# The projection's epilogue: head scales in the rotary tables, squares and normalising straight from PSUM

## The chip, the cores and the metric

The kernel runs on one core of a Trainium2 chip, in float32 throughout. The metric is the device time of one execution in microseconds (us). TensorE is called PE here, its weight loads PEld, VectorE DVE, ScalarE ACT, GpSimd POOL, and SyncE, which only issues DMAs, SP.

## The reference

One layer of an encoder over 1024 tokens and 16 learned meta tokens (1040 rows of 1024 features). What matters here is its first part:

```python
u = _rmsnorm(h, g_attn[l])
proj = u @ w_in[l]                      # 1024 x 2304
qa, ka, va, qd, kd, vd = [proj[..., offs[i]:offs[i + 1]] for i in range(6)]
qa = _rope(_rmsnorm(qa.reshape(B, L, SWA_HQ, SWA_DH), g_q_swa[l]), pos)
ka = _rope(_rmsnorm(ka.reshape(B, L, SWA_HKV, SWA_DH), g_k_swa[l]), pos)
# the same for the 16 q heads and 16 k heads of width 32 of the differential attention
def _rmsnorm(x, g): return x * rsqrt(mean(x * x, -1) + eps) * g       # per head
def _rope(x, pos):  return concat([x1 * cos - x2 * sin, x2 * cos + x1 * sin])   # x1, x2: halves of a head
```

After it come windowed attention, differential attention, the output projection, a router and 32 experts of which each token takes 4. None of that is touched.

## The kernel before, in words

`project` is the first of six stages; a barrier of all engines ends it. Its columns are taken in five groups: 0 is V of the differential attention (512 columns), 1 its Q (512), 2 its K (512), 3 the window attention's Q (512), 4 its K and V (256). An item is one group of columns of one tile of 128 rows; there are 43, numbered 0 to 42 in order: group 0 items 0 to 8, group 1 items 9 to 16, group 2 items 17 to 25, group 3 items 26 to 33, group 4 items 34 to 42. The ninth tile holds the 16 meta rows, and groups 1 and 3 leave it out.

Every product is made of three in single-pass float32: hi x hi, hi x lo, lo x hi (L474 to L476), eight k-tiles, so 24 matmuls an item into one of four PSUM banks `pp`. ACT casts weights to `w_in_hi` (L249) and DVE subtracts to get `w_in_lo` (L327), from four staging buffers that SP fills. The split weights lie in a ring of RING = 14 slots; two groups need 16, so the last LATE = 2 k-tiles of a group can be split only once the group before has used its first ones. `late(i)` says which k-tiles are split beside item i: the first five or six items of a group take one k-tile of the next group each, and a group's first item takes its own late ones too.

An item of groups 1 to 4 then goes through the epilogue, in iterations m of a loop that each engine runs in the same order:

- m = i + 1: ACT copies PSUM to `pr` (L268); POOL squares it into `sq` (L422); DVE sums the squares by head (L343); ACT takes the root (L273); DVE takes the reciprocal (L349) and multiplies `pr` by it into `qn` (L352).
- then POOL multiplies `qn` by the head gains (L430) and, in two halves, by the sine into `t2` (L437). One iteration later on DVE, `rotate` multiplies it in two halves by the cosine into `t1` (L364) and subtracts and adds the halves into `ro` (L370, L371).
- m = i + 3: PE transposes `ro` into `ptq` (L463), up to four blocks, after the products of item m.
- m = i + 4: ACT casts it to `qk_hi` (L282), DVE subtracts to get `qk_lo` (L379), SP stores both (L197).

Each engine works its list in order. DVE's order within an iteration is `qk_lo`, weight tiles, sums, reciprocal, `qn`, `rotate` of the item before. PE waits for `proj_out` before it writes a bank again, four items later.

Of the kernel before, what the change touches and what calls it, by code (L numbers as in the profile page):

```python
# [26 lines left out]
P = 128  # L27
# [48 lines left out]
def project(nc, a, v_all, qk_dram):  # L76

    with ExitStack() as ctx:  # L80
        sb = lambda n, s, d=F32: ctx.enter_context(nc.sbuf_tensor(n, s, d))
        used = []

        def sem(n):
            used.append(nc.alloc_semaphore(n + "_in"))
            return used[-1]

        T = NT + 1
        RAW, RING, GW = 4, 14, 512
        LATE = 2 * KC - RING  # L90
# [22 lines left out]
        ident = sb("ident1", [P, P])  # L113
        pr = sb("pr", [P, 2, GW])
        sq = sb("sq", [P, GW])
# [22 lines left out]
        sq_done, hs_done, hstd_done = sem("head_squares"), sem("head_sums"), sem("head_std")  # L138
        qn_done, gain_done, t1_done, t2_done, ro_done = (sem("qn_done"), sem("gain_done"), sem("t1_done"),
                                                        sem("t2_done"), sem("rotated"))  # L140
        qk_ps, hi_done, lo_done = sem("qk_transposed"), sem("hi_done"), sem("lo_done")
        qk_stored = [sem(f"qk_stored{i}") for i in range(2)]
        dve_chain = sem("dve_chain1")

        def heads(i):

            g, t = items[i]
            c0, c1, at, d, gain = groups[g]
            w = 2 * DH if c0 == KA else c1 - c0
            return rows[t], w, d, gain, (0 if d == DH else 2 * 32)  # L150

        def split_heads(ap, d):
# [21 lines left out]
        def _(sp):  # L174
# [27 lines left out]
            for p in range(RAW):  # L202
                load_w(p)
            load_x(1)
            sp.dma_start(rope[:, 0:NT, :], a["rope"][0:SEQ, :].rearrange("(t p) n -> p t n", p=P)
                         ).then_inc(const_landed, 16)
            sp.dma_start(rope[0:N_META, NT, :], a["rope"][SEQ:KEYS, :]).then_inc(const_landed, 16)
            for i, n in enumerate(("g_q_swa", "g_k_swa")):
# [6 lines left out]
            for p in range(KC, KC + RAW):  # L215
                load_w(p)
            for m in range(NI + 5):
                if m + 3 < T:
                    load_x(m + 3)
                for p in late(m) if m < NI else ():  # L220
                    if p + RAW < NP:
                        load_w(p + RAW)
                if FH <= m - 4 < NI:
                    store(m - 4)
            for i in range(2):
# [3 lines left out]
        def _(act):  # L229
# [27 lines left out]
            def evict(i):  # L257
                g, t = items[i]
                r, w = rows[t], groups[g][1] - groups[g][0]
                act.wait_ge(proj_ps, i + 1)  # L260
                if g == 0:
                    act.copy(v_all[0:r, t, 128:640], pp[0:r, i % 4, 0:512]).then_inc(proj_out, 1)
                else:
                    h = i - FH
                    if h >= 2:
                        act.wait_ge(qn_done, h - 1)
                        act.wait_ge(sq_done, h - 1)
                    act.copy(pr[0:r, h % 2, 0:w], pp[0:r, i % 4, 0:w]).then_inc(proj_out, 1)  # L268

# [21 lines left out]
            norm(1)  # L291
            for m in range(NI + 5):
                if 1 <= m <= NI:
                    evict(m - 1)
                if FH <= m - 4 < NI:
                    high_qk(m - 4)
                if m < NI:
                    g, t = items[m]
                    for p in late(m):
                        high_w(p)  # L300
                    if g == 0:
                        if t + 1 < T:
                            high_u(t + 1)
                        if t + 2 < T:
                            norm(t + 2)
                if FH <= m - 1 < NI:
                    head_std(m - 1)

        @block.vector
        def _(dve):  # L310
            step = chained(dve, dve_chain)
            dve.memset(eps[:, :], EPS).then_inc(consts_set, 1)

# [31 lines left out]
            def normalise(i):  # L345
                r, w, d = heads(i)[0:3]
                h, nh = i - FH, w // d
                dve.wait_ge(hstd_done, h + 1)
                step(dve.reciprocal(hr[0:r, 0:nh], hr[0:r, 0:nh]))  # L349
                if h >= 2:  # L350
                    dve.wait_ge(t2_done, 2 * (h - 1))
                dve.tensor_tensor(split_heads(qn[0:r, h % 2, 0:w], d), split_heads(pr[0:r, h % 2, 0:w], d),  # L352
                                  hr[0:r, 0:nh].unsqueeze(2).broadcast_to((r, nh, d)), ALU.mult).then_inc(qn_done, 1)

            def rotate(i):
                r, w, d, _, c = heads(i)
                h, nh, t = i - FH, w // d, items[i][1]
                dve.wait_ge(gain_done, h + 1)
                if h >= 1:
                    dve.wait_ge(ro_done, 2 * h)  # L360
                q, x, y, o = (split_halves(b, d) for b in (qn[0:r, h % 2, 0:w], t1[0:r, 0:w], t2[0:r, 0:w], ro[0:r, h % 2, 0:w]))
                cos = rope[0:r, t, c:c + d // 2].unsqueeze(1).broadcast_to((r, nh, d // 2))
                for s in range(2):
                    ins = dve.tensor_tensor(x[:, :, s, :], q[:, :, s, :], cos, ALU.mult)  # L364
                ins.then_inc(t1_done, 1)
                dve.wait_ge(t1_done, h + 1)
                dve.wait_ge(t2_done, 2 * (h + 1))
                if h >= 2:
                    dve.wait_ge(qk_ps, h - 1)
                dve.tensor_tensor(o[:, :, 0, :], x[:, :, 0, :], y[:, :, 0, :], ALU.subtract).then_inc(ro_done, 1)  # L370
                dve.tensor_tensor(o[:, :, 1, :], x[:, :, 1, :], y[:, :, 1, :], ALU.add).then_inc(ro_done, 1)  # L371

# [17 lines left out]
            dve.tensor_scalar(gaind[:, 0, :], gaind[:, 0, :], DQ ** -0.5, None, ALU.mult).then_inc(consts_set, 1)  # L390
            for m in range(NI + 5):
                if FH <= m - 4 < NI:
                    low_qk(m - 4)
                if m < NI:
# [8 lines left out]
                if FH <= m - 1 < NI:  # L403
                    head_sums(m - 1)
                    normalise(m - 1)
                if FH <= m - 2 < NI:
                    rotate(m - 2)

        @block.gpsimd
        def _(pool):  # L410
            pool.wait_ge(consts_set, 2)
            pool.wait_ge(const_landed, 16 * 8)

            def squares(i):
                r, w = heads(i)[0:2]
                h = i - FH
                pool.wait_ge(proj_out, i + 1)
                if h >= 1:
                    pool.wait_ge(hs_done, h)
                if items[i][0] == NG - 1:  # L420
                    pool.tensor_copy(v_all[0:r, items[i][1], 0:128], pr[0:r, h % 2, 128:256])
                pool.tensor_tensor(sq[0:r, 0:w], pr[0:r, h % 2, 0:w], pr[0:r, h % 2, 0:w], ALU.mult).then_inc(sq_done, 1)  # L422

            def gain_and_sine(i):
                r, w, d, gain, c = heads(i)
                h, nh, t = i - FH, w // d, items[i][1]
                pool.wait_ge(qn_done, h + 1)
                v = split_heads(qn[0:r, h % 2, 0:w], d)
                table = gains if d == DH else gaind
                pool.tensor_tensor(v, v, table[0:r, gain, :].unsqueeze(1).broadcast_to((r, nh, d)), ALU.mult).then_inc(gain_done, 1)  # L430
                pool.wait_ge(gain_done, h + 1)
                if h >= 1:
                    pool.wait_ge(ro_done, 2 * h)
                q, y = split_halves(qn[0:r, h % 2, 0:w], d), split_halves(t2[0:r, 0:w], d)
                sin = rope[0:r, t, c + d // 2:c + d].unsqueeze(1).broadcast_to((r, nh, d // 2))
                for s in range(2):
                    pool.tensor_tensor(y[:, :, s, :], q[:, :, 1 - s, :], sin, ALU.mult).then_inc(t2_done, 1)  # L437

            for m in range(FH + 1, NI + 5):
                if FH <= m - 1 < NI:  # L440
                    squares(m - 1)
                if FH <= m - 2 < NI:
                    gain_and_sine(m - 2)

        @block.tensor
        def _(pe):
# [36 lines left out]
            transpose_u(0)  # L483
            for m in range(NI + 3):
                if m < NI:
# [3 lines left out]
                    if m >= 4:  # L489
                        pe.wait_ge(proj_out, m - 3)  # L490
                    products(m, 0, KC // 2)
                    if g == 0 and t + 1 < T:
                        transpose_u(t + 1)
                    products(m, KC // 2, KC)
                if FH <= m - 3 < NI:
                    transpose_qk(m - 3)

# [1655 lines left out]
```

## Time and profile before

| | |
|---|---|
| time, median of 3 runs | 2607.39 us (2606.91 to 2609.02) |
| time of the profiled execution | 2607.83 us |
| its span | 2606.2 us |
| PE, DVE, ACT, POOL busy in it | 2335.1, 1924.8, 1451.3, 477.3 us |
| mean granted clock of TensorE | 0.945 of full |
| first 282 us (the projection): PE, DVE, ACT, POOL busy | 246.79, 203.44, 88.12, 126.74 us |

Matmuls overlap in the pipeline, so that PE's busy time doesn't say how near it is to its own rate; the start-to-start time of items in the timeline does. A wait is put down to the instruction that released it last. Instructions of one engine overlap a little, so the time that one takes from its engine is read from start to start.

### The profile page before, as it was taken

How to read it: one execution, taken by the hardware profiler on the slowest of the kernel's cores; microseconds unless marked ns; L12 is line 12 of the kernel's file. 1: busy time of each engine (PE TensorE's matmuls, PEld its weight loads, DVE VectorE, ACT ScalarE, POOL GpSimd, SP SyncE). 2: the span in 40 equal slices, each digit the busy share in tenths (PEclk: the TensorE clock that was granted, in tenths of full speed). 3: DMA queues.
4: the chain of work that ended last, by engine and by line, in shares of the span. 5: the costliest groups of instructions: out<-in, count | busy, mean ns of one | idle time of the engine just before them, and what ended most of it. 6: DMA issues, size and time to landing. Idle time of an engine off the chain costs nothing. (4 is left out here: it accounts for less than half of the span.)

```text
span 2606.2 us, 35142 instructions
## 1 busy us (share of the span) xinstructions
PE 2335.1 (90%) x10673; PEld 1742.3 (67%) x10674; DVE 1924.8 (74%) x2425; ACT 1451.3 (56%) x1694; POOL 477.3 (18%) x546
## 2 busy tenths in 40 slices
PE   6999698999979579999899889999999999988964
PEld 5767565555558457777778677777777777777741
DVE  4699456999956368787775687777777777788767
ACT  4222355888832166676654475656565567667540
POOL 0466100111102311221110011212121111122120
PEclk9999798999989789999999899999999999999985
DMA  4233712332016398797976688877887679799868
GB/s 155 59 108 94 161 40 80 66 66 50 17 45 114 93 337 324 282 348 271 360 254 223 236 318 294 305 256 267 287 311 261 240 277 356 260 353 360 293 242 361
DMA packets 259924, 574.86 MB, mean 221 GB/s; under 512 B 29201, under 2 KB 61329, under 8 KB 254721
## 3 DMA queue, kind: packets, MB, share of 16 engines
q1 hardware_dynamic: 237296, 534.92, 60.3%
q0 software_dynamic: 21056, 34.49, 3.7%
q10 hardware_dynamic: 1488, 4.39, 0.4%
q8 instruction: 46, 0.75, 0.1%
q14 instruction: 38, 0.30, 0.0%
HBM read 548.17 MB, written 60.15 MB: 233 GB/s over the span
## 5 line engine op out<-in xcount | busy, mean ns | idle before, releaser
L1732 DVE TENSOR_TENSOR wlo<-raw,whi 128x2048 fp32r<-128x2048 f32 x387 | 880.6, 2287 | 293.2 <-ACT whi L1628 285.9
L1628 ACT CAST whi<-raw 128x2048 fp32r<-128x2048 f32 x387 | 730.9, 1909 | 227.1 <-PE gl_ps L1900 138.5
L1902 PE MATMUL gl_ps<-whi,xt_hi 128*128 128x512 f32 x1056 | 420.9, 399 | 41.6 <-PEq L1946 24.6
L1904 PE MATMUL gl_ps<-whi,xt_lo 128*128 128x512 f32 x1056 | 414.3, 392 | 0.0
L1903 PE MATMUL gl_ps<-wlo,xt_hi 128*128 128x512 f32 x1056 | 414.1, 392 | 0.0
L1902 PEld LDWEIGHTS gl_ps<-whi,xt_hi 128*128 128x128 f32 x1056 | 199.9, 189 | 93.6 <-issue 25.5
L1904 PEld LDWEIGHTS gl_ps<-whi,xt_lo 128*128 128x128 f32 x1056 | 200.1, 190 | 43.3
L1903 PEld LDWEIGHTS gl_ps<-wlo,xt_hi 128*128 128x128 f32 x1056 | 200.4, 190 | 40.1
L1902 PE MATMUL y_ps<-whi,ht_hi 128*128 128x512 f32 x512 | 215.2, 420 | 0.0
L1903 PE MATMUL y_ps<-wlo,ht_hi 128*128 128x512 f32 x512 | 208.7, 408 | 0.0
L1904 PE MATMUL y_ps<-whi,ht_lo 128*128 128x512 f32 x512 | 208.3, 407 | 0.0
L1562 POOL DMA_INDIRECT xg<-v_dram,idn x67 | 113.6, 1695 | 483.4 <-PE t_ps L1872 403.6
L704 DVE CUSTOM_DVE_ANT_0 e<-s_ps,zero,meta_nm 128x1024 f32<-128x1024 f32 x128 | 163.4, 1277 | 11.8 <-DVE dsb L719 9.9
L1900 PE MATMUL gl_ps<-wlo,xt_hi 128*64 128x512 f32 x416 | 164.7, 396 | 0.0
L1899 PE MATMUL gl_ps<-whi,xt_hi 128*128 128x512 f32 x416 | 162.5, 391 | 0.1
L1602 POOL DMA_INDIRECT y_dram<-ys,idc x64 | 64.0, 1000 | 528.4 <-ACT ys L1672 380.4
L632 ACT ACTIVATE e<-e,nm 128x1040 f32<-128x1040 f32 x128 | 149.1, 1165 | 8.8 <-DVE nm L704 7.9
L474 PE MATMUL pp<-w_in_hi,ut_hi 128*128 128x512 f32 (+3 forms) x344 | 134.6, 391 | 11.2 <-DVE w_in_lo L327 8.8
L817 PE MATMUL o_ps<-pt,v_all 128*64 128x512 f32 (+1 forms) x288 | 139.3, 607 | 0.0
L475 PE MATMUL pp<-w_in_lo,ut_hi 128*128 128x512 f32 (+3 forms) x344 | 130.7, 380 | 0.0
L476 PE MATMUL pp<-w_in_hi,ut_lo 128*128 128x512 f32 (+3 forms) x344 | 129.6, 377 | 0.0
L1649 ACT CAST ht_hi<-t_ps 128x512 fp32r<-128x512 f32 x92 | 45.7, 529 | 128.8 <-PE t_ps L1892 128.4
(262 smaller groups left out, 3954.3 us busy)
## 6 DMA issues: line engine op xcount, KB each, us to landing
raw<-in_w_mlp SPq DMA_DIRECT2D x390, 1024.0 KB, 6.1
b<-in_b_mlp SPq DMA_DIRECT2D x33, 1024.0 KB, 7.7
yk<-y_dram SPq DMA_DIRECT2D x7, 2048.0 KB, 24.7
k_st<-qk_dram SPq DMA_DIRECT2D x32, 260.0 KB, 7.5
xs<-in_x SPq DMA_DIRECT2D x16, 512.0 KB, 4.6
w_in_raw<-in_w_in SPq DMA_DIRECT2D x32, 256.0 KB, 2.9
q_st<-qk_dram SPq DMA_DIRECT2D x32, 256.0 KB, 6.7
qk_dram<-qk_hi SPq DMA_DIRECT2D x24, 256.0 KB, 2.6
```

Of the source, the lines that this page charges most:

```text
L474: pe.matmul(out, ut_hi[:, k, cols(i)], whi[:, s, 0:w], start=(k == 0), stop=False)
L475: pe.matmul(out, ut_hi[:, k, cols(i)], wlo[:, s, 0:w], start=False, stop=False)
L632: act.activation(e[:, n % 2, i, :], e[:, n % 2, i, :], ACT.Exp, bias=nm[:, k:k + 1], scale=-1.0, accum_out=total[:, n % 16, i:i + 1]).then ...
L704: dve.tensor_tensor_reduce(e[:, n % 2, i, 0:SEQ], S(i), zero[:, :], -1.0, meta_nm[:, (n // NT) % 2, at:at + 1], ALU.add, ALU.min, nm[:, k: ...
L817: ins = pe.matmul(o_ps[DV:P, :], vt, pt[0:r, g % 2, c, :], start=(c == 0), stop=(c == 8), skip_group_check=True)
L1628: act.copy(whi[:, k % SPL, :], raw[:, k % RAW, :]).then_inc(hi_done, 1)
L1732: dve.tensor_tensor(wlo[:, k % SPL, :], raw[:, k % RAW, :], whi[:, k % SPL, :].bitcast(F32), ALU.subtract).then_inc(lo_done, 1)
L1899: ins = pe.matmul(bank, xh[:, 1, kc, :], hi, start=start, stop=stop, skip_group_check=True)
L1900: ins = pe.matmul(bank[0:FEW], xh[:, 1, kc, 0:FEW], lo, start=False, stop=stop, skip_group_check=True)
L1902: pe.matmul(bank, xh[:, half, kc, :], hi, start=start, stop=False, skip_group_check=True)
L1903: pe.matmul(bank, xh[:, half, kc, :], lo, start=False, stop=False, skip_group_check=True)
L1904: return pe.matmul(bank, xl[:, half, kc, :], hi, start=False, stop=stop, skip_group_check=True)
```

## The change

The copy to `pr` and the gain product are gone. ACT squares the PSUM bank itself into `sq`, and copies V of the last group from PSUM. DVE multiplies the bank by the reciprocals. POOL builds, once for a group, tables over all nine tiles: cosine times gain and sine times gain, for each head position (four products a table; those of groups 1 and 2 ahead of the loop, those of 3 and 4 behind the sine product of the first item of group 2 and 3). A cosine and a sine product then are one instruction each over all 512 columns, and the subtraction and addition pick the halves. `rotate` moves to the start of DVE's iteration; transposes, casts and stores come one iteration earlier. PE takes `qn` of item m - 4 as the sign that a bank is free. The tables take 9216 bytes a partition, `pr` gave back 4096, and RING goes from 14 to 13, with which LATE becomes 3. DVE sets the 16-row tile of the cosines to zero first, and SP's load into it waits for that.

```diff
...
-RAW, RING, GW = 4, 14, 512
+RAW, RING, GW = 4, 13, 512
...
-pr = sb("pr", [P, 2, GW])
+table = sb("rope_gain", [P, 2, 2, T * DH])
...
-qn_done, gain_done, t1_done, t2_done, ro_done = (sem("qn_done"), sem("gain_done"), sem("t1_done"),
-                                                sem("t2_done"), sem("rotated"))
+qn_done, table_done, t1_done, t2_done, ro_done = (sem("qn_done"), sem("table_done"), sem("t1_done"),
+                                                 sem("t2_done"), sem("rotated"))
...
+rope_set = sem("rope_set")
...
+def rope_gain(i, part):
...
+    r, w, d = heads(i)[0:3]
+    g, t = items[i]
+    return table[0:r, g % 2, part, t * d:(t + 1) * d].unsqueeze(1).broadcast_to((r, w // d, d))
...
+    sp.wait_ge(rope_set, 1)
...
-    for m in range(NI + 5):
+    for m in range(NI + 4):
...
-        if FH <= m - 4 < NI:
-            store(m - 4)
+        if FH <= m - 3 < NI:
+            store(m - 3)
...
-            h = i - FH
-            if h >= 2:
-                act.wait_ge(qn_done, h - 1)
-                act.wait_ge(sq_done, h - 1)
-            act.copy(pr[0:r, h % 2, 0:w], pp[0:r, i % 4, 0:w]).then_inc(proj_out, 1)
+            h, w = i - FH, heads(i)[1]
+            if h >= 1:
+                act.wait_ge(hs_done, h)
+            act.activation(sq[0:r, 0:w], pp[0:r, i % 4, 0:w], ACT.Square).then_inc(sq_done, 1)
+            if g == NG - 1:
+                act.copy(v_all[0:r, t, 0:128], pp[0:r, i % 4, 128:256]).then_inc(proj_out, 1)
...
-    for m in range(NI + 5):
+    for m in range(NI + 4):
...
-        if FH <= m - 4 < NI:
-            high_qk(m - 4)
+        if FH <= m - 3 < NI:
+            high_qk(m - 3)
...
 def _(dve):
...
+    dve.memset(rope[:, NT, :], 0.0).then_inc(rope_set, 1)
...
-            dve.wait_ge(t2_done, 2 * (h - 1))
-        dve.tensor_tensor(split_heads(qn[0:r, h % 2, 0:w], d), split_heads(pr[0:r, h % 2, 0:w], d),
+            dve.wait_ge(t2_done, h - 1)
+            dve.wait_ge(t1_done, h - 1)
+        dve.tensor_tensor(split_heads(qn[0:r, h % 2, 0:w], d), split_heads(pp[0:r, i % 4, 0:w], d),
...
     def rotate(i):
-        r, w, d, _, c = heads(i)
-        h, nh, t = i - FH, w // d, items[i][1]
-        dve.wait_ge(gain_done, h + 1)
+        r, w, d = heads(i)[0:3]
+        h = i - FH
+        dve.wait_ge(qn_done, h + 1)
+        dve.wait_ge(table_done, 4 * items[i][0])
...
-        q, x, y, o = (split_halves(b, d) for b in (qn[0:r, h % 2, 0:w], t1[0:r, 0:w], t2[0:r, 0:w], ro[0:r, h % 2, 0:w]))
-        cos = rope[0:r, t, c:c + d // 2].unsqueeze(1).broadcast_to((r, nh, d // 2))
-        for s in range(2):
-            ins = dve.tensor_tensor(x[:, :, s, :], q[:, :, s, :], cos, ALU.mult)
-        ins.then_inc(t1_done, 1)
+        dve.tensor_tensor(split_heads(t1[0:r, 0:w], d), split_heads(qn[0:r, h % 2, 0:w], d), rope_gain(i, 0), ALU.mult
+                          ).then_inc(t1_done, 1)
+        x, y, o = (split_halves(b, d) for b in (t1[0:r, 0:w], t2[0:r, 0:w], ro[0:r, h % 2, 0:w]))
...
-        dve.wait_ge(t2_done, 2 * (h + 1))
+        dve.wait_ge(t2_done, h + 1)
...
-        dve.tensor_tensor(o[:, :, 0, :], x[:, :, 0, :], y[:, :, 0, :], ALU.subtract).then_inc(ro_done, 1)
-        dve.tensor_tensor(o[:, :, 1, :], x[:, :, 1, :], y[:, :, 1, :], ALU.add).then_inc(ro_done, 1)
+        dve.tensor_tensor(o[:, :, 0, :], x[:, :, 0, :], y[:, :, 1, :], ALU.subtract).then_inc(ro_done, 1)
+        dve.tensor_tensor(o[:, :, 1, :], x[:, :, 1, :], y[:, :, 0, :], ALU.add).then_inc(ro_done, 1)
...
-    for m in range(NI + 5):
-        if FH <= m - 4 < NI:
-            low_qk(m - 4)
+    for m in range(NI + 4):
+        if FH <= m - 2 < NI:
+            rotate(m - 2)
+        if FH <= m - 3 < NI:
+            low_qk(m - 3)
...
-        if FH <= m - 2 < NI:
-            rotate(m - 2)
...
 def _(pool):
...
-    def squares(i):
-        r, w = heads(i)[0:2]
-        h = i - FH
-        pool.wait_ge(proj_out, i + 1)
-        if h >= 1:
-            pool.wait_ge(hs_done, h)
-        if items[i][0] == NG - 1:
-            pool.tensor_copy(v_all[0:r, items[i][1], 0:128], pr[0:r, h % 2, 128:256])
-        pool.tensor_tensor(sq[0:r, 0:w], pr[0:r, h % 2, 0:w], pr[0:r, h % 2, 0:w], ALU.mult).then_inc(sq_done, 1)
...
-    def gain_and_sine(i):
-        r, w, d, gain, c = heads(i)
-        h, nh, t = i - FH, w // d, items[i][1]
+    pool.wait_ge(rope_set, 1)
...
+    def make_table(g):
...
+        d, gain = groups[g][3:5]
+        c, n = (0 if d == DH else 2 * 32), d // 2
+        gains_of = (gains if d == DH else gaind)[:, gain, :]
+        for part in range(2):
+            out = table[:, g % 2, part, 0:T * d].rearrange("p (t s n) -> p t s n", t=T, s=2)
+            for s in range(2):
+                half = gains_of[:, s * n:(s + 1) * n].unsqueeze(1).broadcast_to((P, T, n))
+                pool.tensor_tensor(out[:, :, s, :], rope[:, :, c + part * n:c + (part + 1) * n], half, ALU.mult
+                                   ).then_inc(table_done, 1)
...
+    def sine(i):
+        r, w, d = heads(i)[0:3]
+        h, g = i - FH, items[i][0]
...
-        v = split_heads(qn[0:r, h % 2, 0:w], d)
-        table = gains if d == DH else gaind
-        pool.tensor_tensor(v, v, table[0:r, gain, :].unsqueeze(1).broadcast_to((r, nh, d)), ALU.mult).then_inc(gain_done, 1)
-        pool.wait_ge(gain_done, h + 1)
+        pool.wait_ge(table_done, 4 * g)
...
-        q, y = split_halves(qn[0:r, h % 2, 0:w], d), split_halves(t2[0:r, 0:w], d)
-        sin = rope[0:r, t, c + d // 2:c + d].unsqueeze(1).broadcast_to((r, nh, d // 2))
-        for s in range(2):
-            pool.tensor_tensor(y[:, :, s, :], q[:, :, 1 - s, :], sin, ALU.mult).then_inc(t2_done, 1)
...
-    for m in range(FH + 1, NI + 5):
-        if FH <= m - 1 < NI:
-            squares(m - 1)
-        if FH <= m - 2 < NI:
-            gain_and_sine(m - 2)
+        pool.tensor_tensor(split_heads(t2[0:r, 0:w], d), split_heads(qn[0:r, h % 2, 0:w], d), rope_gain(i, 1), ALU.mult
+                           ).then_inc(t2_done, 1)
+        if i == first_of[g] and 2 <= g < NG - 1:
+            make_table(g + 1)
...
+    make_table(1)
+    make_table(2)
+    for i in range(FH, NI):
+        sine(i)
...
-    for m in range(NI + 3):
+    for m in range(NI + 2):
...
-                pe.wait_ge(proj_out, m - 3)
+                h = m - 4 - FH
+                if h < 0:
+                    pe.wait_ge(proj_out, m - 3)
+                else:
+                    pe.wait_ge(qn_done, h + 1)
+                    if items[m - 4][0] == NG - 1:
+                        pe.wait_ge(proj_out, FH + m - 3 - first_of[NG - 1])
...
-        if FH <= m - 3 < NI:
-            transpose_qk(m - 3)
+        if FH <= m - 2 < NI:
+            transpose_qk(m - 2)
```

## Rows read from the trace of the kernel before

**Rows 1.** The page, parts 1 and 2: busy time, and the clock in 40 slices.

```profile
PE 2335.1 (90%) x10673; PEld 1742.3 (67%) x10674; DVE 1924.8 (74%) x2425; ACT 1451.3 (56%) x1694; POOL 477.3 (18%) x546
...
PEclk9999798999989789999999899999999999999985
```

**Rows 2.** Stretches: length, busy time of PE, PEld, DVE, ACT, POOL, clock, DMA share, GB/s.

```profile
120.00:140.00 20.00, 18.05 (x78) 14.05 (x77) 18.67 (x28) 5.74 (x13) 12.59 (x12) 0.93 0.37 106
...
240.00:260.00 20.00, 15.88 (x110) 15.30 (x109) 18.27 (x37) 5.64 (x14) 13.18 (x21) 0.83 0.36 104
```

**Rows 3.** Waits of PE, 82.9 to 282 us: total us, times, longest.

```profile
PE pp L474 <- DVE w_in_lo L327: 8.8, 5, 4.1
PE ptq L463 <- DVE ro L371: 4.7, 5, 2.6
```

**Rows 4.** Timeline of PE: start us, length us, instruction, idle before it.

```profile
82.91 0.40 PE L474 MATMUL pp<-w_in_hi,ut_hi 128*128 128x512 f32 x1
88.47 0.40 PE L474 MATMUL pp<-w_in_hi,ut_hi 128*128 128x512 f32 x1
...
135.77 0.51 PE L474 MATMUL pp<-w_in_hi,ut_hi 128*128 128x512 f32 x1 [1.79 <-DVE w_in_lo L327]
...
157.66 0.49 PE L474 MATMUL pp<-w_in_hi,ut_hi 128*128 128x512 f32 x1
...
163.67 0.48 PE L474 MATMUL pp<-w_in_hi,ut_hi 128*128 128x512 f32 x1
...
247.63 0.58 PE L474 MATMUL pp<-w_in_hi,ut_hi 128*128 128x256 f32 x1 [4.12 <-DVE w_in_lo L327]
...
254.70 0.36 PE L474 MATMUL pp<-w_in_hi,ut_hi 128*128 128x256 f32 x1
...
257.99 0.36 PE L474 MATMUL pp<-w_in_hi,ut_hi 128*128 128x256 f32 x1
...
260.94 0.37 PE L474 MATMUL pp<-w_in_hi,ut_hi 128*128 128x256 f32 x1
...
275.54 0.74 PE L463 MATMUL ptq<-ident,ro 128*128 128x128 f32 x2
```

**Rows 5.** Timeline of DVE over one period, from reduce to reduce.

```profile
157.65 0.67 DVE L343 TENSOR_REDUCE hs<-sq 128x16 f32<-128x512 f32 x1
...
158.98 0.69 DVE L352 TENSOR_TENSOR qn<-pr,hr 128x512 f32<-128x512 f32 x1
159.59 2.70 DVE L364 TENSOR_TENSOR t<-qn,rope_sb 128x256 f32<-128x256 f32 x2
162.33 0.42 DVE L370 TENSOR_TENSOR ro<-t 128x256 f32<-128x256 f32 x1
...
163.01 0.68 DVE L379 TENSOR_TENSOR qk_lo<-ptq,qk_hi 128x512 fp32r<-128x512 f32 x1
163.61 0.90 DVE L327 TENSOR_TENSOR w_in_lo<-w_in_raw,w_in_hi 128x512 fp32r<-128x512 f32 x1
164.44 0.67 DVE L343 TENSOR_REDUCE hs<-sq 128x16 f32<-128x512 f32 x1
```

**Rows 6.** Timelines: POOL in that period, and DVE's weight tile while POOL idles.

```profile
159.22 1.36 POOL L422 TENSOR_TENSOR sq<-pr 128x512 f32<-128x512 f32 x1 [0.89 <-ACT pr L268]
160.54 1.48 POOL L430 TENSOR_TENSOR qn<-qn,gaind_sb 128x512 f32<-128x512 f32 x1
...
33.69 0.69 DVE L327 TENSOR_TENSOR w_in_lo<-w_in_raw,w_in_hi 128x512 fp32r<-128x512 f32 x1 [1.50 <-ACT w_in_hi L249]
```

**Rows 7.** Groups of ACT by form, 0 to 300 us: busy us, mean ns.

```profile
L268 ACT COPY pr<-pp 128x512 f32<-128x512 f32 x24 | 13.7, 573 | 9.4 <-PE pp L476 9.4
L235 ACT ACTIVATE us<-xs 128x1024 f32<-128x1024 f32 x8 | 8.5, 1059 | 2.1 <-DMA xs<-in_x 2.1
```

**Rows 8.** A group of POOL by form, and the timeline of the last `qk_lo`.

```profile
L430 POOL TENSOR_TENSOR qn<-qn,gains_sb 128x128 f32<-128x128 f32 x8 | 3.9, 483 | 0.0
...
281.42 0.17 DVE L379 TENSOR_TENSOR qk_lo<-ptq,qk_hi 128x16 fp32r<-128x16 f32 x1 [1.16 <-ACT qk_hi L282]
```

## The prediction

> **What bounds the kernel now.** I read the engines' shares first: PE 90%, DVE 74% of the whole span [rows 1]. Those are averages over stages, and the change touches only the first one, the projection, so the next view is the busy time in stretches. In 120 to 140 us DVE is busy 18.67 of 20.00 us, ACT only 5.74, and PE loses 2 us; in 240 to 260 us DVE has 18.27 and PE 15.88, with the clock down to 0.93 and 0.83 of full [rows 2]. So DVE is full and PE has holes. The waits of PE between 82.9 and 282 us say which holes: 8.8 us in 5 waits for `w_in_lo` of DVE L327 and 4.7 us in 5 for `ro` of DVE L371 [rows 3]. Both releasers are DVE instructions: the stage is bound by DVE in its epilogue, and PE pays at the group boundaries, where fresh weights have to be split behind it.
>
> PE's own pace comes from the timeline. An item without head transposes takes 88.47 - 82.91 = 5.56 us, one with four transposes 163.67 - 157.66 = 6.01, a 256-column item 257.99 - 254.70 = 3.29 with four transposes and 260.94 - 257.99 = 2.95 with one [rows 4]. DVE's period comes from two successive reduces: 164.44 - 157.65 = 6.79 us [rows 5]. 6.79 against 6.01 is why DVE lags. PE has four PSUM banks of slack and so feels it only where it catches up: the waits of 1.79 and 4.12 us at 135.77 and 247.63, for instance [rows 4].
>
> **What PE could gain.** Items 9 to 42 and their stalls take 275.54 - 82.91 = 192.63 us [rows 4]. The same PE work in the new order (transposes one item earlier, so from item 11 on) at PE's pace: 2 x 5.56 + 23 x 6.01 + 2 x 3.29 + 7 x 2.95 = 11.12 + 138.23 + 6.58 + 20.65 = 176.58. All that DVE costs PE is 16.05 us. That is more than the 13.5 us of named waits [rows 3], since the granted clock also falls in the two stretches that hold the waits ending at 135.77 and 247.63 [rows 2, 4].
>
> **The change part by part.** DVE's period now, start to start [rows 5]: reduce to `qn` 158.98 - 157.65 = 1.33 (with the square root on ACT in it), `qn` 0.61, the two cosine products 162.33 - 159.59 = 2.74, the two `ro` 163.01 - 162.33 = 0.68, `qk_lo` 0.60, `w_in_lo` 164.44 - 163.61 = 0.83; sum 6.79.
> - *Normalising straight from PSUM.* The row for a 512-column DVE read of PSUM, `qk_lo`, occupies 0.68, and `qn` from SBUF 0.69 [rows 5]: no difference, 0.61 stays. The Trainium skill, "VectorE: DVE Perf Modes", Rules for kernel authors, speaks against this edit: copy PSUM to SBUF first if many operations follow. Here each bank gets two reads by DVE/ACT, and the two rows just named are equal, so that rule would add nothing measurable at this type.
> - *Squares from POOL to ACT, the copy `pr` removed.* On ACT one 512-column pass replaces another. Bounds: 573 ns, the copy from PSUM, and 1059 ns, a Square of 1024 columns [rows 7]; I take 600. ACT is under 30% busy [rows 2], and the square is ready sooner than by copy plus POOL's 1.36 [rows 6]. In the last group a 128-column copy of V is added behind it, under the 0.57 of the wide copy; ACT's idle hides both. Without that cover the square would cost 0.03 us more an item than the copy, and the V copy at most 9 x 0.57 = 5 us.
> - *Cosine product.* Two 256-column products become one of 512. Alone such a product costs 0.61 (as `qn`), the pair of halves 0.68 (as the two `ro`); the present pair takes 2.74 because POOL is active beside it: POOL runs 159.22 to 162.02 [rows 6], and the 0.31 us left after that is nearly half of 0.68. So in 2.43 us beside POOL DVE did about 0.37 us of work, a rate of 0.15. POOL now has one sine product, of the form of its present gain product, 1.48 us [rows 6], and both start at the same `qn`. Estimate: 1.48 us at that rate gives 0.22, the other 0.39 follow: 1.87, say 1.9. Lower end 0.61, upper 2.74; nearer the middle since POOL's 2.8 us of work beside it shrink to about 1.5. The following `ro` wait for POOL's product, which is done by then.
> - *Low weights.* The L327 in rows 5 takes 0.90 beside POOL's sine products of the item before, alone 0.69 [rows 6]; POOL is now idle at that time, so the slot shrinks from 0.83 to 0.62.
> - New period: 1.33 + 0.61 + 1.9 + 0.68 + 0.60 + 0.62 = 5.74 us, 5.12 without a weight tile. Both are under 6.01: **PE becomes the bound**. The removed gain product (POOL 1.48) and one sine product are on no path of the middle.
>
> The Trainium skill, "GPSIMD Engine Reference", Key points, says the SBUF interfaces are shared with VectorE, with contention when a VectorE instruction has two SBUF inputs. By that rule, the trace agrees in the 2.74 us pair; `qk_lo` and the new `qn`, with one input in PSUM, would be spared, which changes no term of the sum.
>
> **What is late next.** With T the end of an item's products, DVE starts `qk_lo` at about T + 1.35 (transposes 0.45, ACT square and hi cast 0.6 each less overlap), and `ro` is complete at T + 1.35 + 5.74 = T + 7.1. PE asks for it after two more items, at T + 12.0: 4.9 us of room. Against it: a group's first item now has four weight tiles (LATE 3, was 2), 3 x 0.62 = 1.9 us; and in groups 2 and 3 POOL builds the next table, four products of 288 columns, by 1.48/512 a column 0.83 us each, 3.3 us together, in which DVE's two-input instructions crawl: 1 to 2.5 us. Sum at most 4.4: inside the room, thinly; if it isn't, each excess shows as a wait of PE for `ro`. The late tiles: PE needs the first of three at T + 0.45 + 15 x 0.23 = T + 3.9, DVE has it at T + 2.6. In the last group (products half as long) it is needed at T + 2.2 and the third at T + 2.9, and they come at T + 2.4 and T + 3.3: 0.5 us, and `ro` of the item before about 0.4 late. I charge 0.9 for this and 1.1 for leftover lag: 16.05 - 2.0 = **14 us** from the loop. The tables of groups 1 and 2 are built near 30 us, long before their use at 95 us; the memset, the wait for it on SP (ahead of it in time by 4 us) and the stores behind it cost nothing. SP's queue sees the same DMAs in the same order, stores one iteration earlier.
>
> **The tail** from the last product to the last `qk_lo` is 281.42 + 0.17 - 275.54 = 6.05 us [rows 4, 8]. Out of it go POOL's gain product (483 ns [rows 8]), one of two sine products, and the copy-then-square pair becomes one pass. That is 0.5, some 0.3 (a quarter of the work of the 483 ns one in two halves, with its fixed part) and up to 0.7; I take 1.5 (bounds 0 and 2.5, as the last hi cast may wait for its buffer's store instead).
>
> Sum: 14 + 1.5 = 15.5 us. The profiled execution took 2607.83 (span 2606.2 and 1.6 around it), the median is 0.44 lower: 2607.4 - 15.5 = **2591.9 us**. Later stages start earlier and are otherwise the same.
>
> **Rivals.**
> 1. *DVE still sets the pace.* If the cosine product beside POOL stays at 2.74, the period is 6.58. For: the only such row. Against: POOL's work beside it halves. DVE then lags 0.6 per weighted item plus 1.9 at boundaries and up to 2.5 for a table, past the room of 4.9 by 2 to 3 us in three groups: gain 15.5 - 8 = 7.5, time 2600.
> 2. *The clock spells stay.* The two dips amount to (1 - 0.93) x 20 and (1 - 0.83) x 20 us of lost clock [rows 2], 1.4 + 3.4 = 4.8. If they come whether PE waits or not, the gain is 10.7: 2596.7. For: the page shows the clock at nine tenths in slices all over the run, busy ones too [rows 1]. Against: here both dips share their stretch with a wait, and nothing in the change adds a pause of PE.
> 3. *Given back later*: the shift of 15 us changes where later dips fall or a DMA bounds the next stage's start. Time within 0.2%, 2603 to 2612.
> 4. *Slower.* DVE, in order, now waits for POOL's sine product of the same item before `ro`, with `qk_lo` and weights queued behind; PE waits for those. It decides from the point where product plus wait exceeds 2.74 + 0.2 = 2.94 (period back at 6.79, with one more late tile), and it costs over 5 us net only from about 3.2 on for all 25 wide items: 25 x 0.26 = 6.5, time 2614. POOL would need twice its 1.48 row for it.
>
> **How the numbers follow.** Forecast 0.57 (own range 2588 to 2595), a yet larger gain 0.04, rival 1 0.16, rival 2 0.13, rival 3 0.06, rival 4 0.04. Range 2587 to 2601. A change under 0.2% (5.2 us) can't be told from none: faster 0.90, same 0.06, slower 0.04.
>
> **What would show it.** Right: item pace of 6.01 from item 11 to 33, no wait of PE for L327 in groups 2 and 3, ACT Square near 0.6, the 512-column cosine product between 1.6 and 2.1, POOL's sine product near 1.5, the stage's last `qk_lo` near 266. Wrong: PE waits for `ro` in each group, a cosine product of 2.7, or a stage end 15 us earlier with the total unmoved.

## The result and the profile after

The changed kernel takes 2591.18 us (median of 4 runs, 2587.86 to 2591.83), the kernel before beside it 2608.2 (2606.91 to 2609.14): ratio 0.9933, 95% interval 0.9915 to 0.995. The forecast was 2591.9 with a range of 2587 to 2601. The median fell by 17.0 us; the profiled spans are 2606.2 and 2589.4 us, 16.8 us apart.

The stretches that held PE's holes [rows 2], in the kernel after: PE is busy throughout, DVE two thirds, and the clock stays at full.

```profile
120.00:140.00 20.00, 20.00 (x94) 16.33 (x93) 13.65 (x26) 6.75 (x14) 5.39 (x3) 1.00 0.46 131
240.00:260.00 20.00, 20.00 (x172) 19.65 (x173) 12.20 (x53) 6.68 (x29) 3.96 (x7) 1.00 0.30 87
```

All waits of PE from 82.9 to 265 us, where there were 8.8 us on weights and 4.7 on `ro` [rows 3]. Of these 3.3 us, 2.6 lie behind the last product (0.21 and 2.41, at 261.27 and 264.01 us). Of the 4.7 before, 3.5 did (2.62 and 0.89, at 278.89 and 280.11 us), so that inside the items the waits fell from 10.0 to 0.7 us:

```profile
PE ptq L473 <- DVE ro L382: 3.3, 3, 2.4
```

PE's timeline, at the places that answer to [rows 4]: the first products of items 9 and 10, of items 22 and 23, of 34, 35 and 36, and the first transposes behind the last product.

```profile
83.22 0.40 PE L484 MATMUL pp<-w_in_hi,ut_hi 128*128 128x512 f32 x1
88.78 0.40 PE L484 MATMUL pp<-w_in_hi,ut_hi 128*128 128x512 f32 x1
...
160.38 0.49 PE L484 MATMUL pp<-w_in_hi,ut_hi 128*128 128x512 f32 x1
...
166.39 0.49 PE L484 MATMUL pp<-w_in_hi,ut_hi 128*128 128x512 f32 x1
...
232.59 0.37 PE L484 MATMUL pp<-w_in_hi,ut_hi 128*128 128x256 f32 x1
...
236.14 0.36 PE L484 MATMUL pp<-w_in_hi,ut_hi 128*128 128x256 f32 x1
...
240.31 0.36 PE L484 MATMUL pp<-w_in_hi,ut_hi 128*128 128x256 f32 x1
...
260.79 0.27 PE L473 MATMUL ptq<-ident,ro 128*128 128x128 f32 x1
```

Items 11 to 33 pass at 6.01 us, PE's own pace. Only the entry of the last group is slower: 3.55 and 4.17 us for items 34 and 35, where 3.29 is the pace. The 0.7 us of waiting that is left inside the items is there, for `ro` at 239.90 us.

DVE's period in the kernel after, and POOL beside it (answers to [rows 5, 6]): the bracket is the idle time before an instruction.

```profile
158.97 0.68 DVE L354 TENSOR_REDUCE hs<-sq 128x16 f32<-128x512 f32 x1
...
160.31 0.69 DVE L364 TENSOR_TENSOR qn<-pp,hr 128x512 f32<-128x512 f32 x1
161.03 0.69 DVE L374 TENSOR_TENSOR t<-qn,rope_gain 128x512 f32<-128x512 f32 x1
162.97 0.43 DVE L381 TENSOR_TENSOR ro<-t 128x256 f32<-128x256 f32 x1 [1.25 <-POOL t L445]
```

```profile
161.08 1.80 POOL L445 TENSOR_TENSOR t<-qn,rope_gain 128x512 f32<-128x512 f32 x1 [4.08 <-DVE qn L364]
```

From `qn` to the next with a weight tile between them it is 160.31 - 154.43 = 5.88 us, without one 5.28. Squares on ACT from PSUM take 0.60:

```profile
L276 ACT ACTIVATE sq<-pp 128x512 f32<-128x512 f32 x24 | 14.4, 599 | 47.4 <-PE pp L486 47.3
```

Where the 16.8 us come from, by the two timelines:

| stretch | before, us | after, us | less |
|---|---|---|---|
| start to item 9 | 82.91 | 83.22 | -0.31 |
| item 9 to the end of the products | 192.63 | 177.57 | 15.06 |
| tail, to the end of the last `qk_lo` | 6.05 | 3.88 | 2.17 |
| to the first matmul of the window attention | 16.41 | 17.21 | -0.80 |
| the rest | 2308.2 | 2307.5 | 0.7 |

Next to nothing was given back. The two small losses lie within what single profiles differ by: in those below item 9 begins anywhere from 81.1 to 84.6 us, and the stretch from the last `qk_lo` to the first matmul of the window attention takes 16.4 to 17.8 us.

### The profile page after: what moved, and what is told of

It is laid out like the page before. It is cut to its first block and busy times, and to the rows that moved or that the text cites. A ratio compares the mean times of both kernels' runs of the same rounds, so it can differ in the third digit from the quotient of the medians.

```text
span 2589.4 us, 34999 instructions
## 1 busy us (share of the span) xinstructions
PE 2328.6 (90%) x10673; PEld 1739.0 (67%) x10674; DVE 1874.4 (72%) x2392; ACT 1452.9 (56%) x1703; POOL 408.1 (16%) x451
```

## The experiments

The later stages, whose code is the same in all of these, differ by up to 6 us between profiles (2305.3 us from the first matmul of the window attention to the end in tables_only, 2311.2 in sine_twice), so the measure is the stage alone, from the first product of item 9 to the end of the last `qk_lo`, each from its one profiled execution. The ratio is to the kernel before as it ran beside each. Its median was 2605.12 us beside psum_only, tables_only, old_order and ring14, 2606.41 beside the next four and 2607.82 beside own_first and after_again, so medians of different groups can't be compared to the microsecond:

| kernel | stage, us | median, us | ratio to before, 95% interval |
|---|---|---|---|
| before | 198.68 | 2608.20 | |
| changed | 181.45 | 2591.18 | 0.9915 to 0.995 |
| psum_only | 182.85 | 2592.99 | 0.9939 to 0.9968 |
| tables_only | 183.43 | 2590.24 | 0.9928 to 0.9956 |
| old_order | 182.04 | 2590.29 | 0.993 to 0.9959 |
| ring14 | 181.17 | 2593.51 | 0.9941 to 0.9969 |
| reduce_once_more | 191.27 | 2600.53 | 0.9969 to 0.9988 |
| sine_twice | 208.62 | 2615.65 | 1.0023 to 1.0048 |
| pe_pause | 194.64 | 2603.57 | 0.9984 to 1.0003 |
| lo_first14 | 183.25 | 2593.93 | 0.994 to 0.9974 |
| own_first | 180.50 | 2589.90 | 0.9916 to 0.9941 |
| after_again | 181.60 | 2591.29 | 0.9924 to 0.9949 |

**psum_only**, one half of the change on the kernel before (the edit shortened; RING stays 14):

```diff
-act.copy(pr[0:r, h % 2, 0:w], pp[0:r, i % 4, 0:w])
+act.activation(sq[0:r, 0:w], pp[0:r, i % 4, 0:w], ACT.Square)
-dve.tensor_tensor(qn, pr, reciprocals)     # POOL's squares go too
+dve.tensor_tensor(qn, pp, reciprocals)
```

> The kernel before with one half of the change: ACT squares the PSUM bank, DVE normalises from it, POOL loses the squares; gain product, sine and cosine halves, RING 14 and the order of the iterations stay as before. Theory (PE is the bound once DVE's period is under 6.01 us): the cosine pair shares the ports with one POOL product instead of two, so DVE's period falls from 6.79 to 1.33 + 0.61 + about 1.95 + 0.68 + 0.60 + 0.83 = 6.0 us and most of the 16 us goes: 2593 to 2597. Rival (the gain is the sum of the two halves, each in proportion to the DVE or POOL work it removes): about half, 2599 to 2601. The first theory also says that the two halves alone add up to clearly more than the 16.8 us of both together.

The median lies at the lower end of the range expected. 15.8 of the 17.2 us of the stage are gone, with the gain product and the halves still there. The cosine pair takes 1.84 us instead of 2.70 [rows 5], beside one POOL product (160.46 to 161.85 us), and ends 0.28 us after it:

```profile
160.29 1.84 DVE L364 TENSOR_TENSOR t<-qn,rope_sb 128x256 f32<-128x256 f32 x2
```

**tables_only**, the other half (tables, whole products; `pr`, POOL's squares and the old order stay; RING 13):

> The kernel before with the other half: gain folded into tables, cosine and sine as one product each (RING 13, LATE 3), but copy to pr, squares on POOL and the old order of the iterations. Theory: the cosine product waits for POOL's square (about 1.0 us) and the weight tile for part of the sine product; period 1.33 + 0.61 + 1.6 + 0.68 + 0.60 + up to 1.1 = 5.9 us, again just under PE's 6.01: 2593 to 2598. Rival (in proportion): 2599 to 2601. If this half did nothing, 2608.

15.3 us are gone. The median, 2590.24, lies 2.8 us under the range expected, which was counted from a kernel before of 2607; beside this run it took 2605.12, 14.9 us more than this kernel. The halves alone give 31.1 us, together 17.2: each brings DVE to about PE's pace, and below that nothing more is to be had. The "in proportion" rival fell in both. DVE and then POOL in this kernel:

```profile
157.56 1.53 DVE L372 TENSOR_TENSOR t<-qn,rope_gain 128x512 f32<-128x512 f32 x1
...
160.41 1.48 DVE L336 TENSOR_TENSOR w_in_lo<-w_in_raw,w_in_hi 128x512 fp32r<-128x512 f32 x1
```

```profile
157.19 1.36 POOL L432 TENSOR_TENSOR sq<-pr 128x512 f32<-128x512 f32 x1 [2.04 <-ACT pr L276]
160.06 1.28 POOL L453 TENSOR_TENSOR t<-qn,rope_gain 128x512 f32<-128x512 f32 x1 [1.51 <-DVE ro L380]
```

The cosine product starts 0.37 us into POOL's square and ends 0.54 after it; the weight tile starts 0.35 into the sine product and ends 0.55 after it. So a DVE instruction with two SBUF inputs that meets a running POOL product does nearly all its work after that one ends. Its period with a weight tile is 6.20 us here, over PE's 6.01, but 4.79 without one, and PE waits only 1.1 us for weights: the room of the pipeline absorbs it.

**old_order**, the changed kernel with `rotate` back at the end of the iteration and transposes one later:

> The changed kernel with the old order: rotate at the end of DVE's iteration, transposes, casts and stores one iteration later. DVE doesn't wait for POOL's sine product then. Theory (PE is the bound, DVE's wait of 1.24 us an item lies inside its slack): loop unchanged at about 177.5 us, tail longer by up to 1.5 us, 2591 to 2593.5. Rival (the reorder was what gained): 2597 or more. Rival (DVE's waits cost something): under 2589.

The stage is 0.6 us longer, but the loop didn't stay as expected. The reorder did two things that nearly cancel. From the last product to the last `qk_lo` this kernel takes 5.46 us where the changed one takes 3.88, so the reorder saved 1.58 us in the tail. From item 9 to the end of the products it takes 176.58 us where the changed one takes 177.57: item 35 passes at 3.28 us instead of 4.17, and PE has no wait inside the items. Here DVE doesn't wait for POOL ahead of `ro`, so the rival that its waits cost something was right by that 0.9 us of item 35. The median lies 0.7 us under the range expected, beside a kernel before that was also faster. POOL's sine product, which now starts when DVE stands idle (it waits for ACT's cast until 160.51 us), takes 1.28 us instead of 1.80:

```profile
159.29 1.28 POOL L445 TENSOR_TENSOR t<-qn,rope_gain 128x512 f32<-128x512 f32 x1 [4.21 <-DVE ro L382]
```

**ring14**, RING 14 and LATE 2:

> The changed kernel with RING 14, LATE 2, as the kernel before had it. Theory: the late tile costs only in the last group, where DVE lags by one tile of 0.4 us: 0.3 to 0.8 us less than the change, 2590 to 2591.5. Rival (late tiles are a cost at every boundary): 2 us less or more, 2589 and below.

The stage is 0.28 us shorter, all of it in item 34 (3.27 us instead of 3.55), just under the 0.3 to 0.8 expected. The median, 2593.51, is above the range expected: in its profile the later stages took 2310.1 us with the same code, 2307.5 in the changed kernel. This is why the stage is the measure.

**reduce_once_more**, to find how much room DVE has:

```diff
+dve.tensor_reduce(spare[0:r, 0, 0:w // d], split_heads(sq[0:r, 0:w], d), AX.X, ALU.add)
 dve.tensor_reduce(hs[0:r, 0:w // d], split_heads(sq[0:r, 0:w], d), AX.X, ALU.add).then_inc(hs_done, 1)
```

> The changed kernel with one spare reduce of 0.61 us an item on DVE. In the changed kernel DVE's period is 5.88 us with a weight tile and 5.28 without (its trace), so over the 25 wide items it needs 25 x 5.28 + 19 tiles x 0.61 + 5 x 0.4 + 2.4 for the tables = 148 us, and PE 150. Theory (PE is the bound by a slack of only some 2 us, and PE has about 5 us of room once): 15.2 us more on DVE cost 15.2 - 2 - 5 = 8 us, up to 12 with the clock: 2598 to 2604, with PE waits for w_in_lo and ro back at the group boundaries. Rival (PE bound with ample slack): under 2593.

9.8 us more in the stage for about 15 us of work on the wide items, and PE's waits inside the items are back:

```profile
PE pp L486 <- DVE w_in_lo L339: 5.2, 2, 2.6
PE ptq L475 <- DVE ro L384: 1.2, 4, 0.4
```

These are 6.4 of the 9.8 us; the rest is about what two stretches of 3.4 us at half the clock cost, 1.7 each (see pe_pause). So the changed kernel lies close to the edge. About 5 of the 15 us cost nothing; how much could be added before the first microsecond is lost, no run shows.

**sine_twice**, POOL's product made twice, the first into a spare tile:

> The changed kernel with POOL's sine product made twice (the first into a spare tile), so that DVE waits for POOL longer. Theory (DVE's and POOL's products exclude each other and DVE stands in the wait with everything behind it): the time from qn to ro grows by 1.2 to 1.3 us, DVE's period to 7.1 with a weight tile, 32 us more over 25 wide items less 7 of slack and room: about 25 us slower than the change, 2612 to 2620, so slower than before: the slow side of the prediction (wait plus product over 2.94 us). Rival (POOL is off the path, its time is hidden): 2590 to 2593.

27.2 us more in the stage (25 were expected), and in all slower than before by 0.23 to 0.48%: the mechanism of the prediction's fourth rival, here made to happen. DVE stands still for 2.50 us ahead of `ro`, with everything behind it:

```profile
158.44 0.69 DVE L375 TENSOR_TENSOR t<-qn,rope_gain 128x512 f32<-128x512 f32 x1
161.63 0.43 DVE L382 TENSOR_TENSOR ro<-t 128x256 f32<-128x256 f32 x1 [2.50 <-POOL t L447]
```

**pe_pause**, two pauses of PE put in:

```diff
-pe.wait_ge(qn_done, h + 1)
+pe.wait_ge(qn_done, h + 4 if m in (17, 34) else h + 1)
```

> The changed kernel with two waits put in on PE: the first item of groups 2 and 4 (17 and 34) waits for qn of the item just before instead of four back, a pause of 5 to 6 us each. Theory (in the kernel before the dips of the clock at 137 and 246 us followed PE's waits): the granted clock falls to the lower level for a few us right after each pause, and the cost is the pauses, 10 to 12 us, plus half of the low stretches, 1.7 to 3.4 each: 2604 to 2609. Rival (the dips have nothing to do with pauses): no low stretch between 35 and 260 us, 2601 to 2603.

The pauses on PE, and the clock granted (third number from the right, a share of 2.4 GHz) in the 8 us after the first and in the 18 after those:

```profile
134.29 0.79 PE L484 MATMUL pp<-w_in_hi,ut_hi 128*128 128x512 f32 x1 [5.80 <-DVE qn L364]
...
242.80 0.58 PE L484 MATMUL pp<-w_in_hi,ut_hi 128*128 128x256 f32 x1 [4.34 <-DVE qn L364]
```

```profile
134.00:142.00 8.00, 7.71 (x28) 6.19 (x29) 1.68 (x4) 0.13 (x1) 1.79 (x1) 0.75 0.38 112
142.00:160.00 18.00, 18.00 (x87) 14.71 (x86) 13.05 (x22) 5.70 (x13) 8.27 (x7) 1.00 0.41 114
```

The stage is 13.2 us longer, 10.1 of them the pauses. Half of the 8 us behind the first ran at 1.2 GHz instead of 2.4, and item 17 took 7.74 us, 1.73 over its pace. Item 34 took 5.29, 1.74 over its 3.55, and item 35 got 0.9 back, as DVE had caught up. The clock fell earlier than expected: from 132 to 134 us, with PE still standing, it was already at 0.50. The median lies between the ranges of the theory and of its rival, but the clock decides: the dips come with PE's pauses, and none came in these stages without one. The changed kernel, both its halves, old_order, ring14 and own_first have none between 35 and 260 us; reduce_once_more, with its waits back, has two of 3.4 us, and sine_twice has three, at its waits of 3.54, 3.56 and 4.90 us for weights. Not every wait brings one: the 2.6 us one of the kernel before at 196 us has none near it. Why that one was spared is open.

**lo_first14**, RING 14 and `qk_lo` ahead of `rotate` on DVE:

> The changed kernel with RING 14 and qk_lo ahead of rotate in DVE's iteration. Theory (exclusion: of a DVE instruction with two SBUF inputs and a POOL instruction, the one that starts first runs at its own pace and the other starts when it ends): POOL's sine product now starts with DVE at qk_lo, which reads PSUM, so it takes its own 1.3 us and not 1.80, the cosine product 0.69, and DVE's wait of 1.24 us is gone; period 5.3 and 4.7. PE is the bound, so the time gains only the stalls of the last group's entry, 0.5 to 1 us: 2589 to 2592. Rival (the sine product on the new table is slow by itself): L445 stays at 1.8. Rival (DVE's waits cost time): under 2588.

This one missed: 1.8 us more in the stage, not less, and 2.1 more than ring14, from which only the order differs. DVE's period did fall to 5.27 us as expected, and POOL's product is at 1.29. The cosine product takes 1.33 and not the 0.69 expected, which again shows that one waits for the other (it ends 0.55 us after POOL's 156.84):

```profile
155.45 0.69 DVE L390 TENSOR_TENSOR qk_lo<-ptq,qk_hi 128x512 fp32r<-128x512 f32 x1
156.06 1.33 DVE L374 TENSOR_TENSOR t<-qn,rope_gain 128x512 f32<-128x512 f32 x1
157.43 0.43 DVE L381 TENSOR_TENSOR ro<-t 128x256 f32<-128x256 f32 x1
```

```profile
155.55 1.29 POOL L445 TENSOR_TENSOR t<-qn,rope_gain 128x512 f32<-128x512 f32 x1 [3.97 <-DVE qn L364]
```

But now `rotate` and the weight tiles stand behind DVE's wait for ACT's cast. At the last group that wait is 2.03 us with `rotate` still to come, where ring14 has `rotate` done and waits 0.70:

```profile
233.61 0.69 DVE L390 TENSOR_TENSOR qk_lo<-ptq,qk_hi 128x512 fp32r<-128x512 f32 x1 [2.03 <-ACT qk_hi L292]
```

The first late weight tile starts at 235.61 us, in ring14 at 234.25, so PE meets late weights there and waits longer for `ro`:

```profile
PE ptq L473 <- DVE ro L382: 3.9, 3, 1.7
PE pp L484 <- DVE w_in_lo L338: 1.1, 1, 1.1
```

I had removed the wait for POOL without asking for what DVE would wait next.

**own_first**, RING 14, and a group's own late tiles split ahead of all else in its first item's iteration, on ACT and on DVE (the edit shortened):

```diff
 for m in range(NI + 4):
+    for p in own(m):          # the late tiles of the group of item m
+        low_w(p)              # high_w(p) on ACT
     if FH <= m - 2 < NI:
         rotate(m - 2)
```

> The changed kernel with RING 14 and a group's own late weight tiles split ahead of everything else in the iteration of its first item, on ACT and DVE, in time in which both wait for PE. Theory (all that is left of DVE's cost to PE is the entry of the last group, 0.26 us in item 34 and 0.88 in item 35): those two items come to 3.3 us each and the stage from item 9 to the last qk_lo takes 180.3 to 180.8 us against 181.45, which the whole time can't tell: 2589 to 2592. Rival (more is hidden in the entries): over 2 us less.

180.50 us: items 34 and 35 take 239.31 - 232.58 = 6.73 us together against 7.72, and PE has no wait left but those behind its last product. The items from 9 on take 176.59 us, and the prediction's sum at PE's own pace was 176.58. It has the shortest stage; its median is 1.4 us under that of the changed kernel run beside it, which those runs can't separate from nothing.

**after_again**, the changed kernel beside own_first:

> The changed kernel once more, beside own_first on one chip, to see how far one kernel moves between chips: stage of 181 to 182 us from item 9 to the last qk_lo, 2588 to 2593.

181.60 us in the stage and 2591.29 in all: in these two profiles the stage repeats within 0.2 us, while the whole times of this kernel's runs spread from 2586.35 to 2593.64.

## Why the prediction was right, step by step

- *DVE bounds the stage; PE's pace is the floor.* Right. The loop gained 15.06 of the 16.05 us that DVE cost PE; 14 were forecast. The halves, own_first and the extra reduce show the floor from both sides. One reading beside it was off: the 13.5 us of named waits [rows 3] were set against these 16.05, but 3.5 of them lie behind the last product, so 10.0 us of waits lie inside, and the low clock and small lags make up the other 6.
- *Normalising from PSUM costs nothing, Square 0.6.* Right: 0.69 and 0.599.
- *The cosine product, 1.9 us beside POOL at a rate of 0.15, with POOL done before `ro`.* The number was right and the mechanism wrong, and two of the signs named for being right didn't come: a cosine product of 1.6 to 2.1 us and a sine product near 1.5. DVE does its product at full pace (0.69), POOL's waits and takes 1.80, and DVE then idles 1.25. Start to start that is 1.94 us. That the sum hardly differs is in part luck: 1.48 us of POOL and a rest of 0.39 on DVE were added up, and what runs one after the other is 0.69 on DVE and 1.28 on POOL. Read again, [rows 5, 6] said so: the pair ended 0.31 us after POOL's second product, about the length of one undisturbed half, which is what a blocked half needs, where I had read a slow rate. The Trainium skill, "GPSIMD Engine Reference", Key points, speaks of contention; these runs show its form for whole products: one waits out the other (1.53 us instead of 0.69 in tables_only).
- *Period 5.74 and 5.12.* Measured 5.88 and 5.28; the weight tile without POOL beside it takes 0.60 of DVE's time, 0.62 was forecast.
- *Leftover lag 1.1 us, last group's entry 0.9.* The first was not there: groups 1 to 3 run at pace, room suffices. The missing 1.1 is the whole miss in the loop. The second was 0.26 + 0.88 = 1.14.
- *The table built in the loop, 1 to 2.5 us of lag.* About 1.2: the two `ro` beside it take 0.96 and 1.03 us instead of 0.42.
- *Tail 1.5.* It was 2.17; the bound of 2.5 held. But the parts were wrong. The 1.5 were the gain product, a sine product and a pass on ACT that go, and the reorder was priced at nothing. By old_order the first came to 0.59 us (6.05 to 5.46) and the reorder to 1.58 (5.46 to 3.88), of which the loop gave 0.99 back.
- *Rival 2, the clock.* Settled by pe_pause: dips come with pauses, and the changed kernel has no pause over 0.7 us inside its items. What they cost was part of the 16.05 all along.
- *Rivals 1 and 4* were a matter of DVE's margin, and that is thin: 1.3 us more on POOL an item made the kernel slower than before.
- *The total.* The forecast took 15.5 us off 2607.4. The kernel before took 2608.2 beside the changed one, and the gain was 17.0: the times agree to 0.7 us, the gains to 1.5.

## What to carry to other kernels

Find the pace of the engine that ought to be the bound, from start to start, and count a gain only down to it: two edits that each get there don't add up. Then ask how far below it the old bottleneck lies now; here 0.6 us an item was enough to lose more than half of the stage's gain. Before moving an instruction forward in an engine's list, ask what it waits for itself and what then stands behind it. A product on POOL beside one on DVE is best counted as one after the other.

## What was not expected of the hardware

- Whichever of the two products starts first runs at its own pace (DVE 0.69 us, POOL 1.28), and the other's time is stretched by what was left of it. In DVE's favour: 0.69 and 1.80 in the changed kernel; in POOL's: 1.29 and 1.33 in lo_first14.
- A table that POOL builds in the loop (four products, 144.03 to 147.95 us in the changed kernel) keeps to the same turns. The first takes 0.80 us, with DVE's `ro` behind it. The two `ro` beside the first and the second take 0.96 and 1.03 us instead of 0.42, each ending 0.3 us after POOL's. The weight tile, 1.6 us after the second `ro`, seems to escape with its plain 0.69, but it starts in the last 0.14 us of the third product, and it is the fourth that is held, 1.25 us instead of 0.80:

```profile
145.05 1.03 DVE L382 TENSOR_TENSOR ro<-t 128x256 f32<-128x256 f32 x1
...
146.60 0.69 DVE L338 TENSOR_TENSOR w_in_lo<-w_in_raw,w_in_hi 128x512 fp32r<-128x512 f32 x1
```

```profile
145.75 0.99 POOL L435 TENSOR_TENSOR rope_gain<-rope_sb,gains_sb 128x288 f32<-128x288 f32 x1
146.70 1.25 POOL L435 TENSOR_TENSOR rope_gain<-rope_sb,gains_sb 128x288 f32<-128x288 f32 x1
```

- A wait of PE can cost more than its length: 5.80 us in pe_pause were followed by 1.73 more at the lower clock, and the clock had fallen while PE still stood.
